# Seven additions of squares, the sparse attention's new order, and moments and zero products in the convolution layer

## The reference

```python
def rmsnorm(x, g):
    xf = x.astype(jnp.float32)
    y = xf * lax.rsqrt(jnp.mean(xf * xf, axis=-1, keepdims=True) + RMS_EPS)
    return (y * g.astype(jnp.float32)).astype(x.dtype)

def swiglu(h, w_gate, w_up, w_down):
    return (jax.nn.silu(h @ w_gate) * (h @ w_up)) @ w_down

def conformer_conv(h, w_pw1, b_pw1, w_dw, b_dw, ln_g, ln_b, w_pw2, b_pw2):
    u = h @ w_pw1 + b_pw1
    a, gate = jnp.split(u, 2, axis=-1)
    u = a * jax.nn.sigmoid(gate)
    u = causal_dwconv(u, w_dw, b_dw)
    u = jax.nn.silu(layernorm(u, ln_g, ln_b))
    return u @ w_pw2 + b_pw2
```

## Time and profile before

| | us |
|---|---|
| median of three runs | 1803.81 |
| lowest and highest | 1802.97 and 1804.19 |
| the profiled execution | 1805.45 |
| its span, first to last instruction | 1803.7 |
| PE busy | 1756.5 (97%) |
| DVE busy | 1291.0 (72%) |
| ACT busy | 988.4 (55%) |
| POOL busy | 501.1 (28%) |

### The profile page before, as it was taken

One profiled execution on the slowest core, in us unless ns is written; L12 is line 12 of the kernel. 1 busy time (PEld: TensorE's weight loads), 2 busy tenths in 40 slices (PEclk: granted clock), 3 DMA queues, 4 the chain that ended last, 5 costly groups with the idle time before them and its releaser, 6 DMA issues.

```text
span 1803.7 us, 36070 instructions
## 1 busy us (share of the span) xinstructions
PE 1756.5 (97%) x14312; PEld 1698.3 (94%) x14312; DVE 1291.0 (72%) x1846; ACT 988.4 (55%) x1469; POOL 501.1 (28%) x504
## 2 busy tenths in 40 slices
PE   5999999999999999999999999999999999999998
PEld 4999999979999999999979999988999999689998
DVE  6787878889777577778966554797666646566665
ACT  4555566574544565446566444676544444854443
POOL 1222200061222232221133211293122184632221
PEclk9999999999999999999999999999999998999999
DMA  9878744628577647676825455422555554135551
GB/s 397 347 275 302 301 164 170 261 107 322 204 267 279 256 176 298 251 279 245 314 94 168 183 185 186 164 94 100 181 186 186 186 179 148 47 119 186 186 186 70
DMA packets 51927, 371.85 MB, mean 206 GB/s; under 512 B 5952, under 2 KB 6208, under 8 KB 6912
## 3 DMA queue, kind: packets, MB, share of 16 engines
q1 hardware_dynamic: 42432, 303.05, 45.8%
q0 software_dynamic: 9408, 67.64, 9.6%
HBM read 368.69 MB, written 1.05 MB: 205 GB/s over the span
## 4 chain that ended last, share of the span: by engine, by line
PE 81%; DVE 8%; ACT 4%; issue 3%; POOL 2%; DMA 2%; SPq 0%; POOLq 0%; DVEq 0%; ACTq 0%
PE gu L867 40%; PE acc L874 8%; PE acc L875 8%; PE acc L876 7%; PE gu L1439 2%; PE gu L874 2%; PE gu L876 2%; PE gu L875 2%; DVE w_lo L2190 2%; DVE mring L2205 2%; PE gu L1271 2%; DMA mring<-in_mods 1%; PE acc L1408 1%; ACT w_hi L1646 1%; POOL arena L830 1%
## 5 line engine op out<-in xcount | busy, mean ns | idle before, releaser
L2190 DVE TENSOR_TENSOR w_lo<-ring,w_hi 128x2048 fp32r<-128x2048 f32 x243 | 565.8, 2331 | 230.8 <-ACT w_hi L1646 230.7
L1646 ACT ACTIVATE w_hi<-ring 128x2048 fp32r<-128x2048 f32 x243 | 463.0, 1907 | 49.9 <-PE acc L876 45.4
L729 POOL TENSOR_TENSOR arena<-arena,rstd 128x512 f32<-128x512 f32 x132 | 210.7, 1596 | 812.1 <-ACT arena L1680 773.2
L867 PE MATMUL gu<-Hs_hi,w_hi 128*128 128x258 f32 (+1 forms) x2080 | 419.3, 283 | 0.7 <-DVE Hs_lo L2251 0.6
L867 PE MATMUL gu<-Hs_lo,w_hi 128*128 128x258 f32 (+1 forms) x2080 | 416.2, 282 | 0.0
L867 PE MATMUL gu<-Hs_hi,w_lo 128*128 128x258 f32 (+1 forms) x2080 | 415.7, 281 | 0.0
L867 PEld LDWEIGHTS gu<-Hs_hi,w_hi 128*128 128x128 f32 x2080 | 320.2, 189 | 1.6 <-DVE Hs_lo L2251 0.8
L867 PEld LDWEIGHTS gu<-Hs_hi,w_lo 128*128 128x128 f32 x2080 | 320.3, 189 | 0.0
L867 PEld LDWEIGHTS gu<-Hs_lo,w_hi 128*128 128x128 f32 x2080 | 320.0, 189 | 0.0
L875 PE MATMUL acc<-hid_lo,w_hi 128*128 128x256 f32 x1056 | 297.8, 282 | 0.0
L874 PE MATMUL acc<-hid_hi,w_hi 128*128 128x256 f32 x1056 | 296.4, 281 | 0.8 <-DVE hid_lo L2377 0.8
(11 more groups left out here) (423 smaller groups left out, 3095.2 us busy)
## 6 DMA issues: line engine op xcount, KB each, us to landing
ring<-in_weights SPq DMA_DIRECT2D x276, 1024.0 KB, 4.8
mring<-in_mods POOLq DMA_DIRECT2D x64, 1024.0 KB, 5.7
mring<-in_mods SPq DMA_DIRECT2D x8, 1024.0 KB, 8.9
con<-in_constants SPq DMA_DIRECT2D x1, 1152.0 KB, 14.6
X<-in_x SPq DMA_DIRECT2D x1, 1024.0 KB, 11.7
out<-X SPq DMA_DIRECT2D x1, 1024.0 KB, 3.9
cact<-in_c SPq DMA_DIRECT2D x1, 512.0 KB, 3.3
arena<-arena POOLq DMA_DIRECT2D x4, 128.0 KB, 2.3
```

Source lines behind the costliest of these rows:

```text
L729: pool.tensor_tensor(both, both, row.unsqueeze(1).to_broadcast([P, 2, L]), ALU.mult).then_inc(scaled_ready, 1)
L867: ins = mm(dst, part, x_lo if i == 1 else x_hi, start=start and i == 0, stop=stop and i == 2, skip_group_check=True)
L1646: act.activation(w_hi[buffer_of(n0, s)][:, :], ring[:, n % RING, :], ACT.Copy).then_inc(hi_ready, 1)
L2190: dve.tensor_tensor(w_lo[b][:, :], ring[:, n % RING, :], w_hi[b][:, :].bitcast(F32), ALU.subtract).then_inc(split_ready, 1)
```

## The change

FFN_ADDS and ADDED become KD − 1 = 7: POOL adds all eight squares, and PE sums with one f32 product (feed-forwards) or two (bare norms, two halves of the tokens). In the convolution layer the moments of tile k − 2 are summed inside slot 0 behind the products of tile k, the last two behind the slot, and eleven products of zeros (`fill`) stand between the waits of the tail. In the sparse attention the eight transposes move into slot 13 behind `first_scores(2)`, into two other banks, ACT copies them ahead of the values of slot 13, PE waits for `pair_free` before the attention's first product with values, and DVE makes the first inverses before the normed diagonal.

```diff
--- before.py
+++ after.py
@@ -509,8 +509,8 @@
         SPLIT_NSA = (0, 1, 2, 3, 6, 7, 10, 11, 12, 13, 14, 15, 16, 17)
         HEAD_ORDER = (2, 3, 1, 0, 4, 5)
 
-        FFN_ADDS = 5
-        ADDED = 4
+        FFN_ADDS = KD - 1
+        ADDED = KD - 1
         BARE_NORMS = ("ssm", "moba", "nsa")
 
         def hidden_tile(s):
@@ -1192,6 +1192,7 @@
                             pe.wait_ge(pair_free, state["free"])
                         if t == 0 and a["cmp"] is not None:
                             pe.wait_ge(cmp_ready, 1)
+                            pe.wait_ge(pair_free, state["free"])
                         pe.wait_ge(pt_ready, base["u"] + t + 1)
                         tile, cmp = a["tile"], a["cmp"]
                         pairs = 1 if cmp is None else 2
@@ -1295,15 +1296,21 @@
                 s0 = state["split"]
                 banks = (gu[:, 0, :], gu[:, 1, :], gu[:, 3, :], acc[:, 3, :])
 
-                def sums():
-
-                    state["sq"] += KD
-                    for m in range(KD):
-                        pe.wait_ge(sq_ready, state["sq"] - KD + m + 1)
-                        for tt in range(2):
-                            ins = mm(stat[:, 2 * tt:2 * tt + 2], early(m)[:, tt * P:(tt + 1) * P], fg2[:, m, :],
-                                     start=(m == 0 and tt == 0), stop=(m == KD - 1), skip_group_check=True)
-                    ins.then_inc(stat_ready, 1)
+                def sums_of(m):
+
+                    state["sq"] += 1
+                    pe.wait_ge(sq_ready, state["sq"])
+                    for tt in range(2):
+                        ins = mm(stat[:, 2 * tt:2 * tt + 2], early(m)[:, tt * P:(tt + 1) * P], fg2[:, m, :],
+                                 start=(m == 0 and tt == 0), stop=(m == KD - 1), skip_group_check=True)
+                    if m == KD - 1:
+                        ins.then_inc(stat_ready, 1)
+
+                def fill(n):
+
+                    for _ in range(n):
+                        mm(acc[:, 3, :], zeros[:, 0:P], zeros[:, 0:1].to_broadcast([P, 512]), start=True, stop=True,
+                           skip_group_check=True)
 
                 def spread_both():
 
@@ -1338,9 +1345,15 @@
                             else:
                                 ins = mm(dst, w[:, cols], early(k), start=(k == 0 and e == 0), stop=(k == KD - 1),
                                          skip_group_check=True)
-                    ins.then_inc(slot_done, 1)
+                        if m == 0 and k >= 2:
+                            if k == KD - 1:
+                                ins.then_inc(slot_done, 1)
+                            sums_of(k - 2)
                     if m == 0:
-                        sums()
+                        sums_of(KD - 2)
+                        sums_of(KD - 1)
+                    else:
+                        ins.then_inc(slot_done, 1)
 
                 def taps(m, t0, t1):
 
@@ -1374,10 +1387,13 @@
                 mean_of(1)
                 taps(7, 16, 31)
                 mean_of(4)
+                fill(1)
                 mean_of(3)
                 mean_of(6)
+                fill(2)
                 mean_of(7)
                 mean_of(5, last=True)
+                fill(2)
                 for m in (0, 1, 2, 3, 4, 6):
                     if m < 4:
                         pe.wait_ge(sq_ready, state["sq"] + m + 1)
@@ -1388,7 +1404,9 @@
                                  start=(m == 0 and tt == 0), stop=(m == 6), skip_group_check=True)
                 ins.then_inc(stat_ready, 1)
                 state["sq"] += KD
+                fill(2)
                 spread_root()
+                fill(4)
                 for j in range(4):
                     if 8 + j in SPLIT_CONF:
                         pe.wait_ge(split_ready, s0 + SPLIT_CONF.index(8 + j) + 1)
@@ -1500,6 +1518,18 @@
                         rows = slice(k % 2 * HD, (k % 2 + 1) * HD)
                         ins = mm(bank[rows, 0:L], z[:, k, :], w, start=(k < 2), stop=(k >= 14), skip_group_check=True)
                     ins.then_inc(slot_done, 2)
+
+                def turn_shares():
+
+                    pe.wait_ge(vcmp_ready, 1)
+                    pe.wait_ge(pair_free, state["free"])
+                    pe.wait_ge(cmp_shared, 1)
+                    for g in range(4):
+                        bank = misc if g >= 2 else up[:, (state["free"] - 1) % 2, :]
+                        for tt in range(2):
+                            ins = pe.transpose(bank[:, (2 * (g % 2) + tt) * P:(2 * (g % 2) + tt + 1) * P],
+                                               pc[:, tt, g * P:(g + 1) * P], ident)
+                    ins.then_inc(cmp_turned, 1)
 
                 def turn_compressed(s, c):
 
@@ -1572,15 +1602,8 @@
                 ins.then_inc(cmp_scored, 1)
                 project(12, values=True, within={2: lambda: spread(4), 4: lambda: head_sums(5),
                                                  6: lambda: first_scores(0), 7: lambda: spread(5)})
-                project(13, values=True, within={2: lambda: first_scores(1), 6: lambda: first_scores(2)})
-                pe.wait_ge(vcmp_ready, 1)
-                pe.wait_ge(pair_free, state["free"])
-                pe.wait_ge(cmp_shared, 1)
-                for g in range(4):
-                    for tt in range(2):
-                        ins = pe.transpose(up[:, g // 2, ((g % 2) * 2 + tt) * P:((g % 2) * 2 + tt + 1) * P],
-                                           pc[:, tt, g * P:(g + 1) * P], ident)
-                ins.then_inc(cmp_turned, 1)
+                project(13, values=True, within={2: lambda: first_scores(1),
+                                                 6: lambda: (first_scores(2), turn_shares())})
                 attention(units, UNITS["nsa"], Pb_nsa, NSA_START)
                 state["split"] = s0 + SPLIT_NSA.index(14)
                 project_parts(n0, 14, O_hi, O_lo)
@@ -2119,10 +2142,11 @@
                 values(n0 + 12, 0)
                 raise_scores(0, UNITS["nsa"], Pb_nsa, negated=True)
                 raise_scores(1, UNITS["nsa"], Pb_nsa, negated=True)
+                act.wait_ge(cmp_turned, 1)
+                for a, bank in enumerate((up[:, (state["free"] - 1) % 2, :], misc)):
+                    ins = act.activation(PC[:, 2 * a:2 * a + 2, :].rearrange("p g t -> p (g t)"), bank, ACT.Copy)
+                ins.then_inc(cmp_ready, 1)
                 values(n0 + 13, L)
-                act.wait_ge(cmp_turned, 1)
-                act.activation(PC.rearrange("p g t -> p (g t)"), up[:, :, :].rearrange("p a t -> p (a t)"),
-                               ACT.Copy).then_inc(cmp_ready, 1)
                 raise_scores(2, UNITS["nsa"], Pb_nsa, negated=True)
                 attention(pairs_nsa(), UNITS["nsa"], Pb_nsa, out=n0, started=NSA_START)
                 split(17)
@@ -2867,6 +2891,7 @@
                 dve.tensor_copy(kcmp, acc[:, 2, 0:30]).then_inc(kcmp_ready, 1)
                 split(11)
                 split(12)
+                inverses(0, 4)
                 dve.wait_ge(kcmp_ready, 1)
                 dve.wait_ge(kcroot_ready, 1)
                 link(dve.reciprocal(kroot[:, 0:30], kroot[:, 0:30]))
@@ -2880,7 +2905,6 @@
                         op0=ALU.mult, op1=ALU.mult)
                 ins.then_inc(kdiag_ready, 1)
                 dve.wait_ge(kdiag_ready, 1)
-                inverses(0, 4)
                 take(6, 10, KS)
                 dve.wait_ge(hidv_ready, 1)
                 hr = hidr.rearrange("p m (g r n) -> p m g r n", g=4, r=4)
```

## The result

The changed kernel took 1808.55 us (median of 17 runs, 1806.64 to 1811.85) against 1803.91 us before (17 runs, 1800.77 to 1805.44): a ratio of 1.0028, 95% interval 1.0020 to 1.0035, so 4.6 us slower. The profiled execution took 1807.29 us.

A forecast was written before the change was run, and what follows sets the result against it. TensorE, busy 97% of the span, was taken as the bound. Additions +6.5, clock +2.5, convolution front −1.0, tail −0.6, sparse attention −1.1 and −1.1 gave +5.2 us on the median 1803.81: 1809.0 us, range 1799 to 1815.

The forecast's parts named there:

- The additions end behind L2190: Entries of slot 1: POOL's last additions take turns with DVE's L2190, so PE's sums come late; +6.5 us in all.
- The second condition of slot 1: Slot 1 also needs its low-half weights from DVE's L2190, so ffn1 and ffn2 can't start sooner even with free additions.
- Late feed-forwards nearly free: ffn3, cffn0, cffn1: longer slot 0 covers the late additions; nothing in ffn3, together +0.1 us in cffn0 and cffn1.
- The clock: PE's idle gaps of 2.2 to 2.5 us in five early entries may halve its clock; +2.5 us, between 0 and 8.5.
- Rival 3: Every gap in the five early entries drops PE's clock: +8.7 us, 1812.5 us; chance 0.15.
- The convolution layer: Small records inside slot 0 keep the clock, −1.0 us; products of zeros in the tail keep it there, −0.6 us.
- The sparse attention: Earlier inverses close PE's 1.1 us wait, −1.1 us; moved transposes and copies close its 1.0 us gap, −1.1 us.
- The sum: Whole kernel: additions, clock, convolution front and tail, and two attention gaps add to +5.2 us, 1809.0 us.
- Rival 2: Additions hidden: POOL is not held by L2190 and addition 7 ends before slot 0; about 1796 us; chance 0.17.
- rival 4: DVE goes first: L2190 gets the port before addition 6, 2.3 us more in eight places, 1825 us; chance 0.04.
- Rival 1: Additions cost PE time but the clock stays in all or nearly all entries: +2.7 us, 1806.5 us; chance 0.20.

The follow-up runs named there:

- fill_gaps: The changed kernel with products of zeros ahead of PE's waits for the last addition in bare norms, ffn1, ffn2, ffn3 and cffn0: 1803.53 us.
- half_low: The kernel before with FFN_ADDS and ADDED at 7 and DVE's L2190 of slot 1 cut into two halves: 1811.65 us.
- no_adds: The changed kernel with FFN_ADDS back at 5 and ADDED at 4: 1796.22 us, ratio 0.9963 to the kernel before.
- ffn_only: no_adds with FFN_ADDS at 7 alone: 1800.31 us.
- only_conf: The kernel before with the convolution layer's part of the change alone: 1798.72 us, ratio 0.9977.
- bare_only: no_adds with ADDED at 7 alone: 1803.03 us.

## Why the prediction was right

1809.0 us was forecast, 1808.55 measured. Step by step:

- **The additions end behind L2190.** Right: 0.5 us (0.54) that L2190 loses, 0.60 (0.58) behind it for the addition, PE idle 2.0 to 2.3 us in five entries. The sum of 6.5 us stands against 7.4 by the medians and 6.3 by the traces. ffn2's entry cost 1.5 in the changed kernel (1.3 in fill_gaps) where 1.3 was forecast: from the start of L2190 to slot 1 it was 3.80 us instead of 3.7, and L2190 began 0.1 later in the layer. The sum rested on one row, L837's 2.77 us.
- **The second condition of slot 1**, that L2190 ends there anyway, decided only in cffn1 (0.23 us), since elsewhere the additions came later still. half_low shows that the condition is real: with the addition 1.06 us sooner slot 1 gains 0.35 at ffn2 and waits for the low half.
- **Late feed-forwards nearly free.** Right: 0.1, 0.2 and −0.3 by fill_gaps and no_adds.
- **The clock.** 2.5 us forecast, 4.0 measured: the term was too small. I had a third of a chance on each of five gaps with 1.7 us each; that is 2.8, not the 2.5 that I put in the sum. Two of five fell in the profiled execution, as forecast in number, but moba's lasted 6.8 us, and all three bare norms fell in one run or another. Rival 3 was added up wrongly: five drops at 8.5 us give +11.2 and 1815.0, the upper edge of the range, and not +8.7 and 1812.5. It is out all the same: in four traces with seven additions in the feed-forwards the clock stayed up behind ffn1 and ffn2, in ffn_only behind a gap of 2.33 us. What the Trainium skill says in "TensorE: Matmul & The Clock Gate", section "HAM oscillation — how this bites in real kernels", is told there of longer waits for DMAs in a loop, and the forecast read it more widely than it is written. For single gaps of 2 us these traces decide, with both outcomes.
- **The convolution layer.** −1.6 forecast, −4.3 measured alone. The mechanism was right in both places, and the size was read from one execution that had the mild form (3.4 us in the front and one stretch in the tail). Others had 6.8 us and two stretches. That the first fills may be too few to keep the clock, as the forecast feared, happened in the profile of only_conf.
- **The sparse attention.** −2.2 forecast, −2.5 measured, 2.4 in the traces.
- **The sum.** By the medians it is +7.4 + 4.0 − 4.3 − 2.5 = +4.6 us where +5.2 was forecast. The cost of the additions was 0.9 us and that of the clock 1.5 us too small in the forecast, the gain of the convolution layer 2.7 us and that of the attention 0.3 too small. The two pairs nearly cancel: the mechanisms were right, but an error of 0.5 us in the time is luck in part.
- **Rival 2** (additions hidden) is excluded by every trace with seven additions, where only cffn1's were hidden; **rival 4** (DVE first) too, addition 6 was let in each time. **Rival 1** (no clock loss, +2.7) is what fill_gaps made: +0.6, and lower than +2.7 because the gain in the convolution layer is 2.7 larger and the waits cost 0.9 more.

## What to carry to other kernels

Work taken from the busiest engine is lost again when its replacement ends behind the point where that engine arrives: ask of each added step which long instruction of the neighbour on the same memory port it will meet, and add what is then left of that instruction, which was nearly all of it here. Choose the number of offloaded steps for each place by when the last input comes (four in the bare norms, five or six in the feed-forwards here), not one number for all. A cost that comes from the clock is different from one execution to the next, so read it from several runs before it goes into a sum, and put products of zeros into gaps that can't be closed, which gave 4.0 us here.

## What the runs showed of the hardware

A gap of 2.0 us in a bare norm was followed by half clock in at least one profiled execution at each of the three places, the gap of 2.3 us in ffn1 in none of four; in half_low a gap of 1.0 us in ssm and moba was followed by it too. The mean granted clock of 0.9968 in bare_only and 0.9993 in ffn_only says the same of the two kinds over 12 and 11 runs. Products of zeros with bf16 operands count as work for the clock: with them in the gaps (fill_gaps) it stayed at 1.00. In the changed kernel's 17 runs the time follows the mean clock: 1806.6 to 1809.2 us at 0.996 and 0.997, 1808.6 to 1809.8 at 0.995, 1811.2 to 1811.9 at 0.993 and 0.994. In the changed kernel the last addition ended 0.58 or 0.59 us behind the DVE operation that it met in eight entries, which agrees with the Trainium skill, "GPSIMD Engine Reference", section "1. Specifications", on the shared SBUF interfaces. That an addition waits for the end of the DVE operation, and isn't slowed in proportion, is what half_low shows, and cffn1 shows the other order: there the DVE operation waited for the addition that had begun 0.06 us ahead of it.
